# Identity products on TensorE at the start of five stages of a decoder layer

## The reference, cut to what matters

```python
xn = rms_norm(x, norm_mix)
q_a, k_a, v_a, q_r, k_r, v_r, g_r, gate_a, gate_r = split(xn @ w_in)
attn = banded_sink_attention(q_a, k_a, v_a, ...)
ret, s_new = retention_branch(q_r, k_r, v_r, g_r, s0, pos0)
merged = sigmoid(gate_a) * (attn @ w_branch_attn) + sigmoid(gate_r) * (ret @ w_branch_ret)
x = x + merged @ w_out
x = x + hierarchical_moe(rms_norm(x, norm_ffn), ...)   # top-1 of 4 groups, top-2 of its 8 experts
y = rms_norm(x, norm_final)
```

## Time and profile before

| | |
|---|---|
| median of 3 runs | 2033.64 us (2032.97 to 2033.86) |
| the profiled execution | 2030.74 us |
| its span, first to last instruction | 2029.2 us |
| PE busy | 1836.7 us (91%) |
| DVE busy | 1156.0 us (57%) |
| mean granted clock of TensorE | 0.946 of full speed |

### The profile page before, as it was taken

One profiled execution on the slowest core, in us unless ns is written; L12 is line 12 of the kernel. 1 busy time (PEld: TensorE's weight loads), 2 busy tenths in 40 slices (PEclk: granted clock), 3 DMA queues, 4 the chain that ended last, 5 costly groups with the idle time before them and its releaser, 6 DMA issues. The chain is left out here.

```text
span 2029.2 us, 29000 instructions
## 1 busy us (share of the span) xinstructions
PE 1836.7 (91%) x9856; PEld 1575.2 (78%) x9856; DVE 1156.0 (57%) x1866; ACT 874.8 (43%) x1535; POOL 493.4 (24%) x464
## 2 busy tenths in 40 slices
PE   7989997999998999999997988976999999999950
PEld 5877774999998878788885987855888888888840
DVE  4256656311111243434334444667999999999937
ACT  4245555321111222222211213345877878778724
POOL 3022323000000121203021001221675333333314
PEclk9989999999998999989997998988999999999985
DMA  7111201222213102020111453347999999999946
GB/s 190 52 48 43 53 22 42 84 67 90 63 58 106 44 25 83 21 82 24 28 58 43 139 157 117 110 174 262 391 388 384 383 386 384 385 388 390 386 172 243
DMA packets 186052, 332.99 MB, mean 164 GB/s; under 512 B 36721, under 2 KB 118033, under 8 KB 184897
## 3 DMA queue, kind: packets, MB, share of 16 engines
q1 hardware_dynamic: 163840, 277.48, 38.3%
q0 software_dynamic: 21328, 53.27, 7.4%
q10 hardware_dynamic: 816, 1.38, 0.4%
HBM read 304.04 MB, written 46.35 MB: 173 GB/s over the span
## 5 line engine op out<-in xcount | busy, mean ns | idle before, releaser
L2062 POOL DMA_INDIRECT y_d<-e_y,e_idxs x32 | 135.6, 4239 | 202.0 <-DVE e_y L2161 200.4
L2132 DVE TENSOR_TENSOR e_Lg<-e_rawg,e_Hg 128x1024 fp32r<-128x1024 f32 x128 | 148.4, 1218 | 6.7 <-ACT e_Hg L2085 6.3
L2132 DVE TENSOR_TENSOR e_Lu<-e_rawu,e_Hu 128x1024 fp32r<-128x1024 f32 x128 | 147.7, 1213 | 0.0
L2132 DVE TENSOR_TENSOR e_Ld<-e_rawd,e_Hd 128x1024 fp32r<-128x1024 f32 x124 | 143.1, 1212 | 0.0
L2085 ACT ACTIVATE e_Hg<-e_rawg 128x1024 fp32r<-128x1024 f32 x128 | 124.9, 1050 | 4.9 <-PE bank L150 4.9
L148 PE MATMUL bank<-r_wH,xH 128*128 128x512 f32 (+1 forms) x288 | 121.0, 420 | 6.3 <-DVE r_wL L1268 3.6
L2085 ACT ACTIVATE e_Hu<-e_rawu 128x1024 fp32r<-128x1024 f32 x124 | 121.0, 1059 | 0.0
L2085 ACT ACTIVATE e_Hd<-e_rawd 128x1024 fp32r<-128x1024 f32 x124 | 121.0, 1049 | 0.0
L150 PE MATMUL bank<-r_wH,xL 128*128 128x512 f32 (+1 forms) x288 | 116.1, 403 | 0.0
L149 PE MATMUL bank<-r_wL,xH 128*128 128x512 f32 (+1 forms) x288 | 115.7, 402 | 0.0
L1030 DVE TENSOR_TENSOR b_wL<-raw,b_wH 128x1024 fp32r<-128x1024 f32 x24 | 29.2, 1221 | 148.4 <-ACT b_wH L1003 148.4
(11 more groups left out here) (390 smaller groups left out, 4841.3 us busy)
## 6 DMA issues: line engine op xcount, KB each, us to landing
e_rawg<-in_w_gate SPq DMA_DIRECT2D x128, 512.0 KB, 12.2
e_rawu<-in_w_up SPq DMA_DIRECT2D x128, 512.0 KB, 10.4
e_rawd<-in_w_down SPq DMA_DIRECT2D x124, 512.0 KB, 11.9
raw<-in_w_in SPq DMA_DIRECT2D x51, 512.0 KB, 3.9
c_Y<-y_d SPq DMA_DIRECT2D x8, 1024.0 KB, 13.2
gate_t<-b_gr_s POOLq DMA_DIRECT2D x8, 528.0 KB, 3.0
m_t<-b_m_s POOLq DMA_DIRECT2D x8, 528.0 KB, 3.5
m_gate<-gate_t POOLq DMA_DIRECT2D x8, 528.0 KB, 4.1
```

The lines of the kernel that those rows point to most:

```text
L2062: pool.indirect_dma_start(out=ch.y_d, out_offset=bass.IndirectOffsetOnAxis(ap=idx[:, e % IDX, 1:2], axis=0), in_=y[:], in_offset=None, bou ...
L2132: dve.tensor_tensor(L[kind][:, q], raw[kind][:, q], H[kind][:, q].bitcast(F32), ALU.subtract).then_inc(w_lo[kind], 1)
```

## The change

A helper is added, and called in the PE function of four stages; in `stage_out` it is called at three places, of which the last stands ahead of the experts. Each call issues `count` products of the 128 x 128 identity with itself into bank 3. No other engine reads the result, and no semaphore is incremented.

```diff
+def keep_busy(pe, bank, ident, count):
+    for _ in range(count):
+        pe.matmul(bank[:, 0:P], ident[:], ident[:], start=True, stop=True)
...
 stage_branch_attn, @block.tensor
+                keep_busy(pe, banks[3], ch.ident, 8)
                 with pe.Fori(0, KT // 2) as j:
...
 stage_retention, @block.tensor
+                keep_busy(pe, banks[3], ch.ident, 30)
                 def body(h, last):
...
 stage_merge, @block.tensor
+                keep_busy(pe, banks[3], ch.ident, 30)
                 def product(s, m, ready=None):
...
 stage_out, @block.tensor
+                keep_busy(pe, banks[3], ch.ident, 24)
+
                 def project(t, f):
...
                         count(t - 2)
+                pe.wait_ge(add_done, NT - 1)
+                keep_busy(pe, banks[3], ch.ident, 16)
                 turn(NT - 1)
                 count(NT - 2)
                 route(NT - 1)
...
                 pe.matmul(banks[2][:, 0:NE], ones[0:NS, :], both[0:NS, NB % 2], start=False, stop=True).then_inc(total_mm, 1)
+                keep_busy(pe, banks[3], ch.ident, 60)
```

## The result

The changed kernel takes 2037.88 us (median of 11 runs, 2036.44 to 2041.46), the kernel before, run beside it, 2032.97 us (11 runs, 2030.94 to 2036.06). The ratio is 1.0026 with a 95% interval of 1.0016 to 1.0035: 4.9 us slower, where the forecast was 4.8 us slower, at 2038.4. The profiled execution of the changed kernel took 2041.37 us with a span of 2039.8 and is one of the longest of the eleven; that of before took 2030.74, less than any of its eleven. So the two traces differ by 10.6 us and the medians by 4.9, and the traces have to be read stage by stage.

What follows compares the result with a forecast made beforehand. PE was taken to bound branch, merge, out and retention's first two products, DVE's splitting the experts. Terms +3.8 + 3.4 - 0.5 - 1.0 + 0 + 0.8 - 2.2 = +4.3, rounded to +4.8: 2038.4 us, range 2034.6 to 2041.6.

Steps and rivals of the forecast that it cites:

- Price of a product: In every added block, one identity product costs 0.224 us at full clock and 0.43 us at half clock.
- When the clock rises: At stage starts, the clock reaches 1.0 after 4.8 us of gapless work, the mean of four half-clock stretches.
- Retention, +3.8: Start of retention: 30 products make PE's first product 6.6 us late, 2.8 us come back at full clock; net +3.8 us.
- Merge, +3.4: Start of merge: 30 products make PE's first product 5.3 us late, 1.9 us come back; net +3.4 us.
- Out, 24, 16 and 60: Out: 24 at the start -0.5 us, 16 ahead of the last transposes zero, 60 ahead of the barrier +0.8 us.
- Branch, -1.0: Start of branch: eight products fit into the 2.4 us wait and may keep the clock up; -1.0 us.
- Experts, -2.2: Start of experts: stage begins at full clock, so transposes and the first eight matmuls run faster; -2.2 us.
- The sum: Whole kernel: all terms together +4.3 us against the profiled execution, rounded to +4.8 us for the median.
- B: All blocks: an identity product costs only what a transpose costs, 0.213 and 0.109 us; -5.6 us, 2028.0 us; chance 0.06.
- C: All blocks: added work is not counted as activity, the clock does not rise; +36 us, 2070 us; chance 0.04.
- S: Rival added with the experiments: added instructions cost something by themselves, through loading of code; no chance given.
- D: Retention or merge: the starting delay is taken up later, or clock dips less often; no change, 2034 to 2036 us; chance 0.14.

Runs made afterwards that it cites:

- the cut kernel: Kernel before plus all six blocks with counts 8, 5, 8, 15, 16, 52 instead of 8, 30, 30, 24, 16, 60: 2025.93 us, ratio 0.9963.

## Why the prediction was right

The sign and the mechanism held: 168 products of about 0.22 us, of which the two blocks of 30 do not fit between the barrier and DVE's split. The size held too, but with luck in the sum, and one term, the experts', was more than twice what was measured. By its steps:

**Price of a product.** 0.224 us at full clock was taken from the plain F32 products of other stages. Measured in the blocks it is 0.223, and two records for each product, as said. The figure of 55.6 ns in the Trainium skill's "TensorE: Matmul & The Clock Gate" (it stands in the section "Wait — 56ns, not 53.3ns?") is for bfloat16, and four times too low for these F32 products, as the trace of before had it.

**When the clock rises.** I took 4.8 us, the mean of four stretches. It rose after 3.2 and 2.9 us in retention and merge, so both blocks took 8.1 to 8.2 us instead of 9.0. Both lie below the bounds of 3.4 to 6.2 us, by 0.2 and 0.5. Elsewhere it rose after 2.9 us (30 in retention alone), 5.2 (30 in merge alone) and 5.7 (60). The moment moves from run to run.

**Retention, +3.8** (+3.0 to +5.7): +2.8 in the changed kernel, just under the bounds, +4.2 with the block alone. **Merge, +3.4** (+1.8 to +4.5): +2.5 and +3.6. DVE's split was not late next, as said. The two blocks alone cost +3.5 and +2.6 us by their ratios, 6.1 against the 7.2 forecast.

**Out, 24, 16 and 60, -0.5 + 0 + 0.8 = +0.3**: +0.34 with all of the change, +0.9 with these three alone. 24 took 7.0 us instead of 7.7; the 16 were hidden; the 60 took 16.4 us instead of 15.7 and brought PE last to the barrier, as said, at a cost of about 1.4 us. **Branch, -1.0** (-1.6 to +1.0): -1.5; with the eight the clock stayed at 1.00, and all six kernels that have them, as products or transposes, took 289.2 us in branch (five of the other six traces 290.7, the sixth 291.9).

**Experts, -2.2** (-2.5 to -1.0): -0.9, outside the bounds. This is the mis-sized term. The step said that the stage begins at full clock and that the eight matmuls up to 1388.8 would then take 0.22 us each. The transposes did run at full clock, but at 1395.9, in the 1.57 us of waiting for DVE behind them, the clock fell, and seven matmuls ran at half. The wait alone does not explain it, for the cut kernel has the same one and no fall. When it does not fall, the stage is 2.2 us shorter: the arithmetic was right, its condition was not sure. A fall behind the transposes should have had a price as a case of its own.

**The sum.** The stages' starts and the unmoved stages of the profiled execution give -1.5 + 2.8 + 2.5 + 0.3 - 0.9 = +3.2 us; the medians say +4.9, with an interval of +3.3 to +7.1. The steps forecast +4.3 and these windows show +3.2, so the agreement of +4.8 with +4.9 is luck in part: clock dips in attention and in the heads move by as much as the largest of the terms between traces.

**Rivals.** B (2028.0 us) has its mechanism shown, but for transposes. C falls: the clock rose in every block of 24 or more that began at half clock, in products and transposes alike. S, which the prediction did not have, falls with the cut kernel. D falls: nothing takes a delay up later.

**What stays open.** What makes one head of retention 5 us longer than another in one run and not in the next: the trace shows a half-clock stretch, not its cause. Why the same wait is followed by a fall of the clock in one kernel and by none in another (2.69 us in retention, 1.57 us in the experts). Whether the products at the experts' start (six) or ahead of the barriers are worth anything beyond the cut counts: with the cut kernel these are four, their medians lie within 0.9 us, and each has other counts in out besides.

## What to carry to other kernels

Work added to keep the clock up has to end before the real work is ready, and what counts is the wait behind the last barrier, not the idle time that the profile puts in its bracket: here 2.5 us of 9.3. Price one filler from a row of the same type and shape at both clock levels, count how many fit, and take fewer: with 5, 8, 15 and 52 products this kernel was 7.5 us faster, where 30, 30, 24 and 60 in the same places made it 4.9 slower. Then look at the next waits on the same engine, since a clock that was raised may be lost again there: behind 1.57 us in one kernel here, kept over 2.69 us in another. And a filler ahead of a barrier has to end before the other engines get there, or it holds up all of them.

## What the runs showed of the hardware

- TensorE's granted clock rose from 0.5 to 1.0 behind 4.5 us of transposes through the identity, as it did behind 2.9 to 5.7 us of plain products; at full clock a transpose of 128 columns of F32 leaves one record of 0.11 us, a product two.
- The clock fell in 3.0 us of idle time behind more than 6 us of work at full clock. The same wait of 2.7 us at the start of retention was followed by a fall in eight traces and by none in four, and that of 1.57 us at the start of the experts by a fall in the changed kernel and in the one with the calls of out alone, and by none in the cut kernel.
- What no edit touched moves by as much between traces as the change is worth: attention by 3.7 us and one head of retention by 6.2 us, the runs of one kernel by 5 us (2030.94 to 2036.06 before, 2036.44 to 2041.46 after).
